# Layer norm of a decoder trunk: the last quarter of seven norms moves from VectorE to ScalarE, and the exponential's table load moves ahead of the copies of the turned tokens

## The chip, the cores and the metric

The kernel runs on one core of a Trainium2 chip. The metric is the device time of one execution in microseconds; of several runs the median counts.

## The reference

Input is x of 256 tokens by 1024 channels in float32. Four layers follow one another. Layer i mixes the tokens (kind i mod 3: gated DeltaNet, differential attention, chunked gMLP, and DeltaNet again in the fourth layer), then a grouped top-2 mixture of 16 experts follows. Each of the eight halves ends in a residual and a layer norm:

```python
def layer_norm(x, g, b):
    mu = jnp.mean(xf, -1, keepdims=True)
    var = jnp.mean(jnp.square(xf - mu), -1, keepdims=True)
    return (xf - mu) * lax.rsqrt(var + EPS) * g + b
...
    h = layer_norm(DN_ALPHA * h + y, ln_mix_g[i], ln_mix_b[i])
    m = grouped_moe(h, w_router, router_bias, e_w1[i], e_w3[i], e_w2[i])
    h = layer_norm(DN_ALPHA * h + m, ln_ffn_g[i], ln_ffn_b[i])
```

The router takes the sigmoid of h times `w_router` per expert, chooses two experts in one group, and the experts are SiLU-gated: `silu(t @ w1) * (t @ w3) @ w2`. All weights are float32; those of one layer's experts are 16 x 3 matrices of 2 MB.

## The kernel before, in words

The 256 tokens lie on the partitions as two tiles of 128 (`tt` 0 and 1), each 1024 channels wide, in the buffer `H`. The eight layer norms are numbered by phase: phases 1, 3, 5 and 7 follow the mixers (called mixer norms here), phases 2, 4, 6 and 8 follow the experts (expert norms). Phase 8 writes the output and has its own code.

A norm is worked in four quarters: two token tiles by two halves of 512 channels. VectorE (DVE) gathers the statistics of a tile (`bn_stats`, L1109 and L1163, then `bn_aggr`, L1116, which signals `var_ready`). ScalarE (ACT) takes the square root (L783 in `ln_rstd`, signal `rstd_ready`). DVE turns it into the reciprocal root with four one-column operations (`root`, L1126 to L1130), each of which waits for the one before through `own.link`. Then `normalise` (L1146) computes (x - mean) * rstd for the two halves. In mixer norms it reads `H` with a stride of 8 elements and writes `XH`, with the channels in another order. In expert norms tile 0 is normalised in place in `H`, and tile 1 is read from the PSUM banks 6 and 7 (where the last expert pass left it) and written to `H`; the signal is then `drained[6]` or `drained[7]` in place of `xhat_ready`.

TensorE (PE) turns the normalised tokens, 128 channels at a time, into the eight banks `ht` (`ht_chunks`; transposes of L1766 in mixer norms and L1754 in expert norms). It waits for a signal at channel chunk 0 and at chunk 4 of each tile. ACT (L764) empties the even chunks and DVE (L1103) the odd ones into `HT`; both multiply by the gain and add the bias of the norm on the way. All of a norm's `HT` is what the next matmuls read.

After a mixer norm the experts stage begins with the router. PE multiplies `HT` by the router weights (L2080, 16 matmuls, each chunk k waiting for the copy of chunk k), ACT copies the result (`rtq`) to SBUF (L1008), PE folds it (L2085), ACT takes the exponential (L1009), and DVE chooses the experts (from L1450 on). SyncE (SP), which issues the weight loads, waits for `rtq` as well ahead of a load into `HT` (L540). ACT's order in this stretch is written out by hand: `ln_rstd(TT)` with a throw-away Sqrt that brings in Sqrt's table (`ahead(ACT.Sqrt)`, L771), the two square roots, `ht_chunks`, then `experts`, which starts with `ahead(ACT.Exp)`: the load of the exponential's table and a throw-away Exp on one column (`warm`), which the next instruction waits for.

After the choice of experts, DVE and PE select the tokens of each expert and PE gathers them (L2099). GpSimd (POOL) writes the normalised tokens out to HBM in the chosen order, and SP brings them back (L572) before it issues further expert weights into slots as PE lets go of them.

After expert norm 2 (the attention layer is next) ACT issues three DMAs in `toeplitz()` between `ln_rstd` and `ht_chunks` (L1000 and twice L1003). They bring the position bias, for which PE waits (`toep_in`) at its first matmul of L1988, in the middle of the attention's input projection (L1775).

Of the kernel before, what the change touches and what calls it, by code (L numbers as in the profile page):

```python
# [22 lines left out]
P = 128  # L23
# [231 lines left out]
def trunk(nc, w, out, kinds=ALL_KINDS, with_moe=True):  # L255
# [3 lines left out]
    with ExitStack() as ctx:  # L259
# [167 lines left out]
        rstd_ready = sem("rstd_ready")  # L427
        xhat_ready = sem("xhat_ready")
        h_ready = sem("h_ready")
        mask_ready = sem("mask_ready")  # L430
        sel_ready = sem("sel_ready")
        spread_set = sem("spread_set")
# [180 lines left out]
        def _(pool):  # L613
# [14 lines left out]
            def residual(phase, which, i):  # L628
                nonlocal ph
                ph += 1  # L630
                pool.wait_ge(rows_in, 32 * ph)
                if phase == last_phase:

                    return
                own.then(pool.tensor_scalar(gB[:, :], gB[:, :], ALPHA, None, ALU.mult))  # L635
                pool.tensor_scalar(bB[:, :], bB[:, :], ALPHA, None, ALU.mult).then_inc(rows_scaled, 1)
                if which and with_moe:

                    pool.wait_ge(spots_ready, i + 1)
                    for n in range(2):  # L640
                        for tt in range(TT):
                            pool.indirect_dma_start(choice_rows, bass.IndirectOffsetOnAxis(ap=spots[:, n * TT + tt:n * TT + tt + 1], axis=0),
                                                    XH[:, tt, :], None).then_inc(rows_out, 16)
                    return
                pool.wait_ge(rows_scaled, ph)
                own.wait()
                if not which:

                    for k in range(KC):
                        wait_data(pool, "ht", phase, k)  # L650
                else:
                    pool.wait_ge(xhat_ready, 6 * i + 4)
                for tt in range(TT):
                    if which:
                        own.then(pool.tensor_tensor(H[:, tt, :].rearrange("t (p k) -> t k p", k=KC), XH[:, tt, :].rearrange("t (k p) -> t k p", k=KC),
                                                    gB[:, :].rearrange("t (p k) -> t k p", k=KC), ALU.mult))
                    else:
                        own.then(pool.tensor_tensor(H[:, tt, :], H[:, tt, :], gB[:, :], ALU.mult))
                own.wait()
                for tt in range(TT):  # L660
                    pool.tensor_tensor(H[:, tt, :], H[:, tt, :], bB[:, :], ALU.add).then_inc(h_ready, 1)
# [68 lines left out]
        def _(act):  # L730
# [41 lines left out]

            rsq = 0

            def ln_rstd(parts=1):

                nonlocal rsq
                ahead(ACT.Sqrt)
                for n in range(parts):
                    ts = slice(n, n + 1) if parts == TT else slice(0, TT)  # L780
                    rsq += 1
                    act.wait_ge(var_ready, rsq)
                    a(rs[:, 0, ts], mv[:, ts, 1], ACT.Sqrt, bias=epsc[:, 0:1]).then_inc(rstd_ready, 1)  # L783

            def heads_root(nn, tt):

# [217 lines left out]
                                  bass.AP(tensor=scratch.tensor, offset=off, ap=[[1, P], [TOEP, HEADS], [1, n]])).then_inc(toep_in, 16)  # L1004

            def experts(i):
                ahead(ACT.Exp)
                emptied(a(logitT, wait_data(act, "rtq", i)[:, 0:SEQ], ACT.Copy), "rtq", i)  # L1008
                emptied(a(rt[:, 0, :], wait_data(act, "rt", i)[:, 0:TT * E], ACT.Exp, scale=-1.0), "rt", i)  # L1009
                wait_copy(act, "rank", i)  # L1010
                first = at[("moe", i)]
                def pair(it, lead):
                    more = GATHER_STEPS if lead else 0
                    counted = [act.value_load(counts[0:1, bass.ds(it * 2 + j, 1)], min_val=0, max_val=SEQ) for j in range(2)]
                    def turned(j):

                        b = 2 + j
                        act.wait_ge(filled[b], it * 3 + (first[b] + 2))
                        a(hT[j], bank[b][:, SEQ:].rearrange("p (m c) -> p m c", m=4), ACT.Copy).then_inc(drained[b], 1)  # L1019

                    for j in range(2):
                        b = 2 + j
                        if j and not lead:
                            turned(0)
                        act.wait_ge(filled[b], it * 3 + (first[b] + 1))
                        a(sil[j][CAP:, :], bank[b][0:CAP, :], ACT.Silu).then_inc(silu_h, 1)  # L1026
                        with act.If(counted[j] > CAP):
                            with act.Fori(1, PASSES) as n:
                                with act.If(counted[j] > n * Q + Q):
                                    b0 = act.snap(steps_done)  # L1030
                                    act.wait_ge(baton, b0 + (more + 2))
                                    a(m_sil[CAP:, 0:SEQ], bank[5][0:CAP, 0:SEQ], ACT.Silu).then_inc(baton, 1)
                                    act.wait_ge(baton, b0 + (more + 5))
                                    a(m_turned[:, 0:SEQ + P], bank[6][:, 0:SEQ + P], ACT.Copy).then_inc(baton, 1)
                                    act.wait_ge(baton, b0 + (more + 7))
                                    a(m_y, bank[7][:, :], ACT.Copy).then_inc(baton, 1)
                                    act.reg_add(steps_done, steps_done, PASS_STEPS + more)
                    for j in range(2):
                        if lead or j:
                            turned(j)  # L1040
                        if lead and j == 0:
                            for k in range(1, KC, 2):
                                ps = wait_data(act, "cg", i, k)
                                if k > 1:
                                    wait_data(act, "cg", i, KC - 1)
                                c = KC * i + k
                                emptied(a(xc[:, k, 0:2 * SEQ], ps[:, :], ACT.Identity, scale=lncols[:, c:c + 1], bias=lncols[:, c + 32:c + 33]), "cg", i, k)
                    for j in range(2):
                        b = 2 + j
                        act.wait_ge(filled[b], it * 3 + (first[b] + 3))  # L1050
                        for nh in range(2):
                            ins = a(y_[CAP * j:CAP * (j + 1), nh * 512:(nh + 1) * 512], bank[b][nh * CAP:(nh + 1) * CAP, :], ACT.Copy)  # L1052
                        ins.then_inc(drained[b], 1)

                pair(0, True)
                with act.Fori(1, E // 2) as it:
                    pair(it, False)
# [6 lines left out]
            for i, kind in enumerate(kinds):  # L1064
                j = kinds[:i].count(kind)
                if kind == 0:
                    delta(i, j, nn)
                    nn += 1
                elif kind == 1:
                    attention(i, j)  # L1070
                    for tt in range(TT):
                        heads_root(nn, tt)
                        heads_out_T(i, tt, lambda n: bOT[:, :, n * P:(n + 1) * P])
                    nn += 1
                else:
                    gmlp(i, j)
                rows_load(2 * i + 1, 1, i)
                ln_rstd(TT)
                if 2 * i + 1 != last_phase:
                    ht_chunks(2 * i + 1)  # L1080
                if with_moe:
                    experts(i)
                    rows_load(2 * i + 2, 0, i)
                    ln_rstd(TT)
                if 1 in kinds[i + 1:i + 2]:
                    toeplitz()
                if i < n_layers - 1:
                    ht_chunks(2 * i + 2)
# [3 lines left out]
        def _(dve):  # L1092
# [42 lines left out]

            def normalise(phase, tt):

                for kh in range(2):
                    dst = src = H[:, tt, kh * 512:(kh + 1) * 512]
                    ready = xhat_ready  # L1140
                    if phase % 2:
# [579 lines left out]
        def _(pe):  # L1721
# [21 lines left out]
            def ht_chunks(phase):  # L1743
                if phase and phase % 2 == 0:
                    i = phase // 2 - 1
                    for tt, ks in ((0, range(6)), (1, range(6)), (0, (6, 7)), (1, (6, 7))):
                        for k in ks:
                            if tt == 0:
                                pe.wait_ge(xhat_ready, 6 * i + 5 + k // 4)
                                fill("ht", phase, k)  # L1750
                            elif k % 4 == 0:
                                b = 6 + k // 4
# [7 lines left out]
                for tt in range(TT):  # L1760
                    if phase == 0:
                        pe.wait_ge(x_ready[tt], 16)
                    for k in range(KC):
                        if phase and k % 4 == 0:
                            pe.wait_ge(xhat_ready, 6 * (phase // 2) + 2 * tt + k // 4 + 1)
                        ins = tr(pss[k][:, tt * P:(tt + 1) * P], src[:, tt, k * P:(k + 1) * P], ident)  # L1766
                        if tt == TT - 1:
                            done(ins, "ht", phase, k)
# [641 lines left out]
```

## Time and profile before

| what | value |
|---|---|
| median of 3 runs | 1864.21 us (1863.75 to 1871.41) |
| span of the profiled execution | 1862.9 us |
| what lies around the span, against the median | 1.3 us |
| PE busy | 1704.4 us, 91% |
| DVE busy | 660.7 us, 35% |
| ACT busy | 456.2 us, 24% |
| POOL busy | 164.6 us, 9% |

The profile is of one execution. Its own total time is not listed apart from the runs', so the span is set beside their median. Starts in the rows are microseconds from the start of the span. "L1146" is a line of the kernel. A busy PE is not PE at its peak. The idle time before an instruction and what released it stand in square brackets.

### The profile page before, as it was taken

How to read it: one execution, taken by the hardware profiler on the slowest of the kernel's cores; microseconds unless marked ns; L12 is line 12 of the kernel's file. 1: busy time of each engine (PE TensorE's matmuls, PEld its weight loads, DVE VectorE, ACT ScalarE, POOL GpSimd, SP SyncE). 2: the span in 40 equal slices, each digit the busy share in tenths (PEclk: the TensorE clock that was granted, in tenths of full speed). 3: DMA queues.
4: the chain of work that ended last, by engine and by line, in shares of the span. 5: the costliest groups of instructions: out<-in, count | busy, mean ns of one | idle time of the engine just before them, and what ended most of it. 6: DMA issues, size and time to landing. Idle time of an engine off the chain costs nothing. (4 is left out here: it accounts for less than half of the span.)

```text
span 1862.9 us, 24394 instructions
## 1 busy us (share of the span) xinstructions
PE 1704.4 (91%) x9154; PEld 880.5 (47%) x9154; DVE 660.7 (35%) x1397; ACT 456.2 (24%) x898; POOL 164.6 (9%) x129
## 2 busy tenths in 40 slices
PE   8998989998898888899999997899989998899986
PEld 7866643332584443333344544333368667433322
DVE  3443563222216552232302225222243435542223
ACT  1674312111204121111211101111124834111111
POOL 1013110000300100000020100000030131200000
PEclk9999989999999989999999998999989999899999
DMA  9431089999943389689974339899993220699996
GB/s 335 178 128 47 24 317 423 421 422 423 386 168 119 109 367 407 269 345 421 403 256 147 113 145 384 369 423 421 423 344 136 91 92 2 250 383 422 422 422 249
DMA packets 107163, 521.87 MB, mean 280 GB/s; under 512 B 10819, under 2 KB 19060, under 8 KB 65788
## 3 DMA queue, kind: packets, MB, share of 16 engines
q1 hardware_dynamic: 93680, 497.05, 66.5%
q10 hardware_dynamic: 11020, 14.07, 2.3%
q0 software_dynamic: 2304, 8.39, 1.1%
q8 instruction: 130, 2.13, 0.5%
q14 instruction: 29, 0.24, 0.0%
HBM read 510.03 MB, written 9.45 MB: 279 GB/s over the span
## 5 line engine op out<-in xcount | busy, mean ns | idle before, releaser
L2112 PE MATMUL bank<-ring,work 128*64 128x512 f32 x1280 | 285.1, 595 | 7.9 <-DMA ring<-in_e_w 7.9
L1618 DVE TENSOR_TENSOR work<-bank,work 64x512 f32<-64x512 f32 x64 | 68.0, 1063 | 530.6 <-ACT work L1026 530.5
L1775 PE MATMUL bank<-HT,ring 128*128 128x256 f32 x1024 | 231.4, 386 | 0.0
L2156 PE MATMUL bank<-ring,work 128*64 128x512 f32 x896 | 206.8, 603 | 12.1 <-DMA ring<-in_e_w 9.8
L1775 PEld LDWEIGHTS bank<-HT,ring 128*128 128x128 f32 x1024 | 198.4, 194 | 37.0 <-issue 10.2
L1783 PE MATMUL bank<-ring,HT 128*128 128x512 f32 x448 | 197.9, 601 | 0.0
L2112 PEld LDWEIGHTS bank<-ring,work 128*64 128x64 f32 x1280 | 88.5, 137 | 176.6 <-issue 160.7
L1026 ACT ACTIVATE work<-bank 64x512 f32<-64x512 f32 x64 | 37.7, 589 | 428.0 <-PE bank L2112 428.0
L1783 PEld LDWEIGHTS bank<-ring,HT 128*128 128x128 f32 x448 | 85.9, 194 | 103.8 <-issue 103.8
L2156 PEld LDWEIGHTS bank<-ring,work 128*64 128x64 f32 x896 | 61.7, 138 | 133.5 <-issue 111.2
L2189 PE MATMUL bank<-work 128*128 128x512 f32 x256 | 119.7, 611 | 5.2 <-DVE H L1641 5.2
L635 POOL TENSOR_SCALAR gB<-gB 128x1024 f32<-128x1024 f32 x7 | 20.1, 2867 | 1036.1 <-DMA bB<-in_ln_ffn_b 716.6
L1052 ACT ACTIVATE work<-bank 64x512 f32<-64x512 f32 x128 | 75.7, 592 | 130.5 <-PE bank L2156 129.8
L1249 DVE SCALAR_TENSOR_TENSOR work<-bank,convcols,work 128x255 f32<-128x255 f32 x144 | 69.3, 482 | 103.3 <-ACT work L829 99.9
L2112 PE MATMUL bank<-work 128*64 128x512 f32 x320 | 101.0, 593 | 3.8 <-DMA work<-in_e_w 2.7
L1808 PE MATMUL bank<-ring,work 128*128 128x512 f32 x192 | 84.2, 597 | 0.0
L2189 PEld LDWEIGHTS bank<-work 128*128 128x128 f32 x256 | 46.9, 192 | 77.4 <-issue 69.4
L2112 PE MATMUL bank<-early_slot,work 128*64 128x512 f32 x320 | 72.2, 593 | 2.6 <-DMA early_slot<-in_e_w 2.6
L1569 DVE TENSOR_TENSOR H<-bank,H 128x512 f32<-128x512 f32 x112 | 70.1, 684 | 6.3 <-PE bank L2189 5.2
L1019 ACT ACTIVATE work<-bank 128x256 f32<-128x256 f32 x64 | 24.6, 384 | 173.3 <-PE bank L2120 173.2
L2112 PEld LDWEIGHTS bank<-work 128*64 128x64 f32 x320 | 30.9, 137 | 69.3 <-issue 61.1
L2112 PE MATMUL bank<-HT,work 128*64 128x512 f32 x128 | 57.6, 593 | 0.0
(318 smaller groups left out, 1798.1 us busy)
## 6 DMA issues: line engine op xcount, KB each, us to landing
ring<-in_e_w SPq DMA_DIRECT2D x160, 1024.0 KB, 18.5
ring<-in_e_w SPq DMA_DIRECT2D x56, 2048.0 KB, 21.2
early_slot<-in_e_w SPq DMA_DIRECT2D x40, 1024.0 KB, 18.2
work<-in_e_w SPq DMA_DIRECT2D x40, 1024.0 KB, 19.4
ring<-in_a_w_in SPq DMA_DIRECT2D x15, 2048.0 KB, 19.7
HT<-in_e_w SPq DMA_DIRECT2D x16, 1024.0 KB, 20.6
work<-in_e_w SPq DMA_DIRECT2D x8, 2048.0 KB, 22.7
ring<-in_c_w_in SPq DMA_DIRECT2D x8, 2048.0 KB, 22.6
```

Source lines behind the costliest of these rows:

```text
L1019: a(hT[j], bank[b][:, SEQ:].rearrange("p (m c) -> p m c", m=4), ACT.Copy).then_inc(drained[b], 1)
L1026: a(sil[j][CAP:, :], bank[b][0:CAP, :], ACT.Silu).then_inc(silu_h, 1)
L1052: ins = a(y_[CAP * j:CAP * (j + 1), nh * 512:(nh + 1) * 512], bank[b][nh * CAP:(nh + 1) * CAP, :], ACT.Copy)
L1249: ins = v.scalar_tensor_tensor(dst[:, back:SEQ], ps[:, 0:SEQ - back], convcols[:, j, col:col + 1], dst[:, back:SEQ], ALU.mult, ALU.add)
L1569: v.tensor_tensor(part(b), bank[b][:, :], part(b), ALU.add).then_inc(drained[b], 1)
L1618: v.tensor_tensor(by_m(h_[j]), bank[b][CAP:, :], sil[j][CAP:, :], ALU.mult).then_inc(drained[b], 1)
L1775: ins = mm(dst[:, 0:SEQ], wt[:, k, n * P:(n + 1) * P], HT[:, k, :], start=k == 0, stop=k == KC - 1)
L1783: ins = mm(dst[:, :], HT[:, k, tt * P:(tt + 1) * P], wt[:, k, :], start=k == 0, stop=k == KC - 1)
L1808: ins = mm(ps[:, :], turned(h, tt), wts[nh][:, h, :], start=h == 0, stop=h == HEADS - 1)
L2112: ins = mm(bank[b][lo:lo + CAP, :], x[:, k, :], wt[k], start=k == 0, stop=k == KC - 1, skip_group_check=True)
L2156: ins = mm(bank[b][nh * CAP:(nh + 1) * CAP, :], h[:, m, :], w2[m][:, nh * 512:(nh + 1) * 512], start=m == 0, stop=m == 3, skip_group_check ...
L2189: mm(bank[b][:, :], selgT[:, tt * P:(tt + 1) * P], y_[:, nh * 512:(nh + 1) * 512], start=tt not in onto_h, stop=True, skip_group_check=tt ...
```

## The change

For the phases 1 to 7 the last quarter (tile 1, channels 512 to 1023) is normalised by ACT. DVE computes -mean * rstd of tile 1 in one more one-column operation and signals it as `shift_ready`. ACT waits for it and does Identity(x * rstd + shift) over 512 channels right behind the second square root. In mixer norms it signals the new semaphore `xhat_last`, in expert norms `drained[7]`. PE's and POOL's waits are counted anew. The throw-away Exp with its table load moves from the start of `experts` to the place between `ln_rstd` and `ht_chunks` of the mixer norms. Phase 8 stays as it was.

```diff
-            def ln_rstd(parts=1):
+            def ln_rstd(parts=1, phase=None):
...
                     a(rs[:, 0, ts], mv[:, ts, 1], ACT.Sqrt, bias=epsc[:, 0:1]).then_inc(rstd_ready, 1)
+                    if phase is not None and n:
+                        second_half(phase)
+
+            def second_half(phase):
+
+                act.wait_ge(shift_ready, phase)
+                if phase % 2:
+                    dst = XH[:, 1, 512:].rearrange("t (k p) -> t k p", p=P)
+                    src, ready = H[:, 1, :].rearrange("t (p k) -> t k p", k=KC)[:, 4:, :], xhat_last
+                else:
+                    dst, src, ready = H[:, 1, 512:], bank[7][:, :], drained[7]
+                a(dst, src, ACT.Identity, scale=rs[:, 3, 1:2], bias=rs[:, 2, 1:2]).then_inc(ready, 1)
...
             def experts(i):
-                ahead(ACT.Exp)
...
                 rows_load(2 * i + 1, 1, i)
-                ln_rstd(TT)
+                ln_rstd(TT, 2 * i + 1)
+                ahead(ACT.Exp)
                 if 2 * i + 1 != last_phase:
                     ht_chunks(2 * i + 1)
                 if with_moe:
                     experts(i)
                     rows_load(2 * i + 2, 0, i)
-                    ln_rstd(TT)
+                    ln_rstd(TT, 2 * i + 2 if 2 * i + 2 != last_phase else None)
...
             def normalise(phase, tt):

-                for kh in range(2):
+                if tt:
+                    v.scalar_tensor_tensor(rs[:, 2, 1:2], mv[:, 1, 0:1], -1.0, rs[:, 3, 1:2], ALU.mult, ALU.mult).then_inc(shift_ready, 1)
+                for kh in range(1 if tt else 2):
...
                         if phase and k % 4 == 0:
-                            pe.wait_ge(xhat_ready, 6 * (phase // 2) + 2 * tt + k // 4 + 1)
+                            if (tt, k) == (1, 4):
+                                pe.wait_ge(xhat_last, phase // 2 + 1)
+                            else:
+                                pe.wait_ge(xhat_ready, 5 * (phase // 2) + 2 * tt + k // 4 + 1)
```

## Rows read from the trace of the kernel before

**Rows 1.** The page: the span.

```profile
span 1862.9 us, 24394 instructions
```

**Rows 2.** Chain that ended last, phase 7: start us, us, what.

```profile
1607.38 0.75 DVE work L1146
1608.13 0.04 issue
...
1608.69 1.94 ACT HT L764 x4
...
1610.64 1.16 ACT L771
...
1612.17 0.39 ACT work L1008
```

**Rows 3.** Timelines of DVE, ACT and SP in phase 3.

```profile
648.63 0.16 DVE L1130 SCALAR_TENSOR_TENSOR rs<-rs 128x1 f32<-128x1 f32 x1
648.83 1.41 DVE L1146 TENSOR_SCALAR work<-H,mv,rs 128x512 f32<-128x512 f32 x2
650.14 1.90 DVE L1103 TENSOR_SCALAR HT<-bank,lncols 128x256 f32<-128x256 f32 x4
...
649.99 1.93 ACT L764 ACTIVATE HT<-bank,lncols 128x256 f32<-128x256 f32 x4 [1.98 <-PE bank L1766]
651.94 1.28 ACT L771 ACT_TABLE_LOAD   x1
653.47 0.38 ACT L1008 ACTIVATE work<-bank 128x256 f32<-128x256 f32 x1
...
652.74 0.33 SPq L540 DMA_DIRECT2D HT<-in_e_w  x1
```

**Rows 4.** The same timelines in phase 1, and DVE's tile 0 there.

```profile
232.12 2.82 DVE L1146 TENSOR_SCALAR work<-H,mv,rs 128x512 f32<-128x512 f32 x2
...
245.79 1.41 DVE L1146 TENSOR_SCALAR work<-H,mv,rs 128x512 f32<-128x512 f32 x2
247.31 1.90 DVE L1103 TENSOR_SCALAR HT<-bank,lncols 128x256 f32<-128x256 f32 x4
...
250.58 0.38 ACT L1008 ACTIVATE work<-bank 128x256 f32<-128x256 f32 x1
...
250.48 0.33 SPq L540 DMA_DIRECT2D HT<-in_e_w  x1
```

**Rows 5.** Timelines of DVE and SP in phase 7.

```profile
1608.90 1.90 DVE L1103 TENSOR_SCALAR HT<-bank,lncols 128x256 f32<-128x256 f32 x4
...
1611.78 0.33 SPq L540 DMA_DIRECT2D HT<-in_e_w  x1
```

**Rows 6.** Stretches: us, busy of PE, PEld, DVE, ACT, POOL, PEclk, DMA share, GB/s.

```profile
260.00:264.00 4.00, 4.00 (x25) 4.00 (x24) 1.99 (x11) 1.28 (x1) 2.05 (x2) 0.62 0.66 271
...
268.00:272.00 4.00, 4.00 (x22) 1.38 (x20) 2.26 (x15) 0.00 (x0) 0.00 (x0) 1.00 0.60 210
...
272.00:400.00 128.00, 126.01 (x580) 45.44 (x578) 40.72 (x60) 24.35 (x44) 0.00 (x0) 1.00 1.01 420
```

**Rows 7.** Groups of instructions by line, ACT: 512 columns from PSUM, scale and bias per partition.

```profile
L1047 ACT ACTIVATE work<-bank,lncols 128x512 f32<-128x512 f32 x16 | 11.6, 775 | 18.3 <-PE bank L2200 18.3
```

**Rows 8.** Timelines of DVE and PE in phase 2.

```profile
491.46 1.53 DVE L1146 TENSOR_SCALAR H<-bank,mv,rs 128x512 f32<-128x512 f32 x2
...
492.32 2.40 PE L1754 MATMUL bank<-consts_sb,H 128*128 128x128 f32 x10 [1.05 <-DVE H L1146]
```

**Rows 9.** The position bias: ACT's queue, the DMA's landing, PE's first use.

```profile
489.94 0.34 ACTq L1000 DMA_DIRECT2D work<-in_consts  x1
490.31 1.25 ACTq L1003 DMA_DIRECT2D work<-toeplitz_rows  x2
...
work<-toeplitz_rows ACTq DMA_DIRECT2D x1, 1024.0 KB, 20.1
...
512.08 1.02 PE L1988 MATMUL bank<-work 128*128 128x512 f32 x2
```

More of the change, by code:

```diff
@@ L429, in trunk @@
         h_ready = sem("h_ready")
+        shift_ready = sem("shift_ready")
+        xhat_last = sem("xhat_last")
         mask_ready = sem("mask_ready")
@@ L651, in residual @@
                 else:
-                    pool.wait_ge(xhat_ready, 6 * i + 4)
+                    pool.wait_ge(xhat_ready, 5 * i + 3)
+                    pool.wait_ge(xhat_last, i + 1)
                 for tt in range(TT):
@@ L1748, in ht_chunks @@
                             if tt == 0:
-                                pe.wait_ge(xhat_ready, 6 * i + 5 + k // 4)
+                                pe.wait_ge(xhat_ready, 5 * i + 4 + k // 4)
                                 fill("ht", phase, k)
```

## The prediction

> **What bounds the kernel now.** I first read the page for the span, 1862.9 us [rows 1], then the chain of waits that ended last, to see whether a layer norm stands in it and by which instructions. It does. In phase 7 the chain goes from VectorE's quarter (L1146) over PE's turn to ScalarE's four copies (L764), then to the table load (L771), then to the copy of the router's result (L1008) [rows 2]. So ScalarE, not VectorE, is the engine that holds this stretch from the first turned chunk on, and the table load stands in the chain.
>
> The timelines show how much of that load is exposed. L1008 needs two things: the router's last matmul, whose end SP shows (it waits for the same signal ahead of its load into HT), and ScalarE free. In phase 3 the matmuls end at 652.74 and L1008 starts at 653.47: the load costs 0.73 us less a hand-over of 0.04, so 0.69 [rows 2, 3]. Phase 5 repeats phase 3 to within 0.01. In phase 1 it is 250.58 - 250.48 - 0.04 = 0.06 [rows 4], in phase 7 1612.17 - 1611.78 - 0.04 = 0.35 [rows 2, 5]. All four together expose 1.8 us of the 5.1 us that four loads take; the rest lies under the router's matmuls.
>
> Does a delay here reach the end? After the router, the choice of experts, the gather and the return of the gathered rows follow in one chain, and SP lets go of further weights only behind it. DMA is not backlogged then: 0.60 busy in 268 to 272. From 272 on it is full at 420 GB/s [rows 6], and moves the start of that stretch along with the router. I therefore pass every delay on in full, in mixer norms as in expert norms, behind which PE works without a gap.
>
> **The change, part by part.** S is the start of VectorE's third quarter (first of tile 1), right behind the last step of `root`: 245.79, 648.83 and 1607.38 in phases 1, 3 and 7 [rows 2 to 4].
>
> *The added one-column operation.* It is of the kind of L1130, 0.16 us [rows 3]. It stands ahead of the third quarter. VectorE overlaps neighbours a little when none waits: two quarters take 1.41, though one is 0.75, so 0.09 overlap [rows 2, 3]. That gives 0.07 at least, and 0.20 (the pitch from L1130 at 648.63 to 648.83) at most. I take 0.10, nearest the unlinked case that this is. PE's first turn starts that much later.
>
> *The quarter taken off VectorE.* Its end is what PE waits for at chunk 4. In expert norms PE starts the turns at 492.32 and VectorE ends the quarter at 492.99 [rows 8]; ten turns take 2.40, so the four ahead of chunk 4 take 0.96, more than the 0.67 between. In mixer norms ScalarE's copies, 1.93 for four, are slower than the turns that feed them [rows 3]. VectorE's own next work, the odd copies, starts during the quarter's last 0.1 us or right behind it [rows 3, 8] and isn't last. I cost the gain at nothing: under the quarter lie PE's four turns. If they were gone it would be worth 0.66.
>
> *ScalarE's quarter in mixer norms.* It starts at S + 0.16 + 0.04. The trace has no Identity from SBUF with this stride. Nearest is L1047, the same function, width and operands from PSUM: 0.775 [rows 7]. From above, VectorE's quarters of the same strided tile: 0.75, and 1.41 each in their slowest pair (2.82) [rows 4]. I take 0.80, as ScalarE's own row is nearest. It ends at S + 1.00, just ahead of PE's chunk 4. In expert norms, with PSUM as source, 0.775 fits as it stands, and behind it stand only the copies, which wait for PE, and in phase 2 three DMAs (below).
>
> The Trainium skill speaks against the strided read ("SBUF - State Buffer", the notes on SBUF cachelines): accesses that cross to a new 16-byte line pay a penalty, and here each step is 32 bytes. No row shows it for ScalarE.
>
> *The moved table load.* This is the large term. It can't start before ScalarE's quarter is done, and the copies wait behind it: quarter to S + 1.00, load 1.28, then 0.25 to the next instruction (in phase 3 from 651.94 + 1.28 to 653.47) [rows 3]. The first copy starts at S + 2.54 in place of S + 1.16 (649.99 - 648.83). The four copies take 1.93, so the last ends at S + 4.47. Then the router's last matmuls must still run: from the last copy (VectorE's, 652.04) to 652.74 are 0.70 us in phase 3; 1.27 in phase 1 (249.21 to 250.48) and 0.98 in phase 7 (1610.80 to 1611.78) [rows 3 to 5]. L1008 then starts at:
> phase 1: 245.79 + 4.47 + 1.27 + 0.04 = 251.57, later by 0.99;
> phase 3: 648.83 + 4.47 + 0.70 + 0.04 = 654.04, later by 0.57; phase 5 the same;
> phase 7: 1607.38 + 4.47 + 0.98 + 0.04 = 1612.87, later by 0.70.
> Sum 2.8 us. The load that was mostly hidden under the router's matmuls now stands in front of what they need. The bounds are 2 (matmuls catching up) and 3.5.
>
> On the price of a load the Trainium skill ("ScalarE: Activation LUTs", What ACT_TABLE_LOAD costs) gives 1283 ns plus 1380 ns of drain. The trace agrees on the first (1.28) and shows no drain: the next instruction starts 0.25 later, itself included. By the page the sum would be up to 4 x 1.38 = 5.5 us more.
>
> *Expert norms.* Three times the 0.10 ahead of PE's first turn: 0.3.
>
> *Order of ScalarE's queue in phase 2.* The three position-bias DMAs were issued from 489.94 to 491.56. Now they are behind the wait for `shift_ready`: from 491.46 + 0.16 + 0.04 = 491.66, so 1.72 later. They hold up the copies of phase 2 by some 0.4, hidden under the turns still to come. But PE needs the bias at 512.08, and the large DMA, issued between 490.31 and 491.56, takes 20.1 to land: 510.4 to 511.7 [rows 9]. 1.72 later it lands at 512.1 to 513.4. Since PE has slipped by 0.1, the wait is 0 to 1.3; I take the middle, 0.7. Other transfers share the engines then, so it may land less late.
>
> **Sum.** 2.8 + 0.3 + 0.7 = 3.8 us on the span of 1862.9. The median of the runs is 1.3 above the span, so 1864.2 + 3.8 = 1868.0. That is 0.2%. A measurement of this kernel tells about 0.5%, 9.3 us, from no change (the three runs lie 7.7 us apart), so my forecast is no change that shows, leaning to slower.
>
> **The rivals.**
> *The load hides, as the move suggests.* If ScalarE had room for it before PE's first turned chunk is there, the exposed 1.8 would be saved, and VectorE's added operation would still cost 0.3 in the expert norms: 1864.2 - 1.8 + 0.3 = 1862.7. Against it: ScalarE's idle time ahead of the copies is 1.98 us in all [rows 3], but the quarter cuts it in two, and only S + 1.00 to S + 1.16 lies behind the quarter. 0.08.
> *The strided quarter is slow.* 1.41 in place of 0.80 delays load and copies four times by 0.6, and PE's chunk 4 with it: 1870.4. For it the stride; against it the flat rows of ScalarE. 0.12.
> *The delay is absorbed.* The bias lands in time and the router's matmuls catch up: 1865.5. 0.15.
> *Slower by more than shows: the clock.* PE would idle up to 1.4 us more between its turns and the router. In 260 to 264 the granted clock is 0.62, so between half and full speed [rows 6], and phase 1's router tail at 1.27 against phase 3's 0.70 prices a low clock at about half speed. If the low clock lasts longer behind each idle spell, PE's work costs double for as long. To add the missing 5.5 us it must last some 2.8 us longer at each of four norms, with PE busy at half speed in twice that. Against it: the idle time of the expert choice is far longer and decides anyway. 1874 and more. 0.04.
> *It does not do what it says*: another table load for Identity. No: Identity follows Sqrt without one in every norm [rows 3]. Under 0.01.
>
> **How the numbers follow.** My forecast has 0.60; with the absorbed case and the slow quarter 0.87 lies between 1864 and 1872. The range goes from 1862.0, which takes in most of the gain, to 1872.0: the slow quarter, and a long bias wait. Of the three signs: faster by over 0.5% would need 9.3 us, while all four loads and seven quarters together are 5.1 + 5.3 = 10.4; 0.02. Slower by over 0.5%: the clock, and 0.01 for what no row shows, 0.05. Within 0.5%: 0.93.
>
> **What would show it.** In the profile after: ScalarE's quarter of 0.8 us at S + 0.2, the load right behind it, the first copy at S + 2.5, no gap at L1008 other than PE's, and 0.6 to 1.0 more from S to L1008 in the four mixer norms. A wait for DMA at PE's first L1988. I am wrong if the copies start near S + 1.2, if the quarter takes over 1.0, or if the span grows while these intervals don't.

## The result and the profile after

The changed kernel takes 1872.3 us (median of 11 runs, 1870.2 to 1879.4); the kernel before, run beside it, 1866.1 us. The ratio is 1.0032, 95% interval 1.0019 to 1.0046: the change costs 6.0 us (3.5 to 8.6). The spans of the two profiled executions are 5.6 us apart, 1868.5 against 1862.9. The forecast was 1868.0 us, 3.8 us slower, with 1872.0 as the upper end. Sign and place were right, the size was not. (Where a whole time is given in us against before, below too, it is worked out from the ratio of the runs.)

Phase 3 shows the change at work. The line of the span on its profile page and the timelines of VectorE, ScalarE, PE and SP in the changed kernel:

```profile
span 1868.5 us, 24401 instructions
...
653.01 0.16 DVE L1141 RECIPROCAL rs<-rs 128x1 f32<-128x1 f32 x1 [0.36 <-ACT rs L786]
...
653.79 0.16 DVE L1154 SCALAR_TENSOR_TENSOR rs<-mv,rs 128x1 f32<-128x1 f32 x1
653.87 0.73 DVE L1163 TENSOR_SCALAR work<-H,mv,rs 128x512 f32<-128x512 f32 x1
...
653.99 1.31 ACT L798 ACTIVATE work<-H,rs 128x512 f32<-128x512 f32 x1 [1.01 <-DVE rs L1154]
655.32 1.28 ACT L774 ACT_TABLE_LOAD   x1
656.62 0.20 ACT L774 ACTIVATE warm<-epsc 128x1 f32<-128x1 f32 x1
656.85 1.93 ACT L767 ACTIVATE HT<-bank,lncols 128x256 f32<-128x256 f32 x4
659.95 0.38 ACT L1022 ACTIVATE work<-bank 128x256 f32<-128x256 f32 x1 [1.17 <-PE bank L2100]
...
654.66 1.35 PE L1786 MATMUL bank<-consts_sb,work 128*128 128x128 f32 x8 [1.66 <-DVE work L1163]
657.92 1.98 PE L2100 MATMUL bank<-HT,wr 128*32 128x256 f32 x16 [1.91 <-ACT HT L767]
...
659.95 0.33 SPq L542 DMA_DIRECT2D HT<-in_e_w  x1
```

These answer to [rows 3]. Before, the four copies (L764, now L767) started 1.16 us behind S, as soon as PE had turned the first chunk. Now the quarter (L798, 1.31), the load (1.28) and the throw-away Exp stand in front of them, and PE idles 1.91 us between its turns and the router. Where the copy of the router's result used to wait for the load, it now waits 1.17 us for PE.

To compare kernels I measure from R, the start of VectorE's reciprocal for tile 1, to that copy (L1008, now L1022). In phase 3 it is 659.95 - 653.01 = 6.94 us, and it was 653.47 - 648.04 = 5.43. The table gives all kernels that matter; every number in it is a difference of two starts in the timelines of one profiled execution of each kernel, and the last column adds the four norms' differences to before. The kernels of the last three rows have e1's order of ScalarE in their mixer norms.

| kernel | phase 1 | 3 | 5 | 7 | sum against before |
|---|---|---|---|---|---|
| before | 5.57 | 5.43 | 5.43 | 5.57 | |
| changed | 6.95 | 6.94 | 6.94 | 6.95 | +5.8 |
| table load alone (e1) | 5.36 | 4.71 | 4.70 | 5.12 | -2.1 |
| quarter alone (e2) | 5.66 | 5.65 | 5.66 | 5.66 | +0.6 |
| load ahead of the quarter (e4) | 5.94 | 5.94 | 5.93 | 5.93 | +1.7 |
| two more switches (e8) | 9.97 | 9.97 | 9.97 | 9.98 | +17.9 |
| expert quarter alone (e6) | 5.14 | 5.48 | 4.71 | 5.24 | -1.4 |
| GpSimd later (e7) | 5.09 | 5.47 | 4.71 | 5.29 | -1.4 |
| e7 again (e11) | 5.07 | 5.48 | 5.13 | 5.29 | -1.0 |

The chain that ended last in phase 7 has the same order now (changed kernel; start us, us, what):

```profile
1611.50 0.17 DVE rs L1154
...
1611.69 1.06 ACT work L798
1612.75 0.29 issue
1613.04 1.28 ACT L774
1614.32 0.01 issue
1614.33 0.21 ACT warm L774
1614.54 0.03 issue
1614.57 1.03 ACT HT L767 x2
1615.60 0.04 issue
1615.64 2.00 PE bank L2100 x16
1617.64 0.02 issue
1617.67 0.39 ACT work L1022
```

In [rows 2] VectorE's quarter and PE's first turn led to the copies and the load came behind them. Now quarter, load and copies are one series on ScalarE, and the router's matmuls have joined it.

The groups of instructions give ScalarE's quarter by its two forms, from SBUF in the mixer norms and from PSUM in the expert norms (changed kernel: busy us, mean ns of one | idle before):

```profile
L798 ACT ACTIVATE work<-H,rs 128x512 f32<-128x512 f32 x4 | 5.3, 1322 | 4.0 <-DVE rs L1154 4.0
L798 ACT ACTIVATE H<-bank,rs 128x512 f32<-128x512 f32 x3 | 2.3, 777 | 5.6 <-DVE rs L1154 5.6
```

From PSUM it takes 0.777, as [rows 7] had it. From SBUF with the stride it takes 1.32. In phase 4 PE's turns of tile 1 begin 1.71 us behind R, where they began at 1.65: 0.06 for the added operation. Phase 2 lost 0.74 there; that is taken up below.

The 5.8 of the four norms lies close to the 6.0 of the whole time, but two executions don't make a ledger. At R the changed kernel's profile is 9.5 us behind the one of before in phase 5 (1121.79 against 1112.29) and 4.1 in phase 7 (1610.72 against 1606.60). From the one R to the other it took 5.4 us less than before, though its norm of phase 5 alone costs 1.5 more, so other stretches vary by more than the whole change costs. That a norm's delay reaches the end rests on the medians, and on e8.

### The profile page after: what moved, and what is told of

Its sections match the earlier page's. It is cut to its first block and busy times, and to the rows that moved or that the text cites. A ratio compares the mean times of both kernels' runs of the same rounds, so it can differ in the third digit from the quotient of the medians.

```text
span 1868.5 us, 24401 instructions
## 1 busy us (share of the span) xinstructions
PE 1710.0 (92%) x9154; PEld 884.5 (47%) x9154; DVE 656.4 (35%) x1397; ACT 463.6 (25%) x905; POOL 165.1 (9%) x129
## 5 line engine op out<-in xcount | busy, mean ns | idle before, releaser
L1828 PEld LDWEIGHTS bank<-ring,work 128*128 128x128 f32 x192 | 36.8, 195 | 45.1 <-issue 45.1
```

The lines of the kernel that those rows point to most:

```text
L1828: ins = mm(ps[:, :], turned(h, tt), wts[nh][:, h, :], start=h == 0, stop=h == HEADS - 1)
```

## The experiments

Three things were open: whether the moved load, the quarter or something outside ScalarE costs the 6 us; why the quarter takes 1.32; and how much of a delay in a norm reaches the end. Line numbers are those of each kernel; the times of before that were measured beside them are 1867.0 us for e1 to e4, 1867.2 for e5 to e8 and 1865.7 for e9 to e11.

### e1: the table load alone

```diff
                 rows_load(2 * i + 1, 1, i)
                 ln_rstd(TT)
+                ahead(ACT.Exp)
...
             def experts(i):
-                ahead(ACT.Exp)
```

(against the kernel before)

> The kernel before with the table load alone moved; VectorE keeps all quarters. R is the start of VectorE's reciprocal for tile 1 (root); from R to the copy of the router's result (L1008) the kernel before takes 5.57, 5.43, 5.43 and 5.57 us in phases 1, 3, 5 and 7, the changed kernel 6.94 to 6.95 in all four. Theory A (series on ScalarE: whatever stands between the second square root and the copies counts only if it lasts beyond PE's first turned chunk): the load fits into ScalarE's idle time behind the second square root, the copies start as before, and L1008 comes at R + 5.5, 4.75, 4.75, 5.2; four norms save 1.8 us, the time is 0.1% under before. Theory B (the moved load itself is what costs): L1008 at R + 6 or later, time 2 to 6 us above before. Theory C (clock and DMA, not ScalarE's order, made the difference): R to L1008 says nothing, the time is near that of the changed kernel.

1866.2 us, ratio 0.9993 (0.9977 to 1.0008). ScalarE's timeline in phase 3:

```profile
647.21 0.29 ACT L783 ACTIVATE rs<-mv,epsc 128x1 f32<-128x1 f32 x1 [13.38 <-DVE mv L1116]
647.52 1.28 ACT L771 ACT_TABLE_LOAD   x1
648.81 0.20 ACT L771 ACTIVATE warm<-epsc 128x1 f32<-128x1 f32 x1
649.54 1.93 ACT L764 ACTIVATE HT<-bank,lncols 128x256 f32<-128x256 f32 x4 [0.52 <-PE bank L1766]
652.24 0.38 ACT L1007 ACTIVATE work<-bank 128x256 f32<-128x256 f32 x1 [0.77 <-PE bank L2080]
```

The load starts right behind the second square root, and ScalarE is done with it and the throw-away Exp 0.52 us before PE's first turned chunk lets the copies start. L1008 comes at R + 5.36, 4.71, 4.70 and 5.12: 2.1 us saved over four norms in this execution, where 1.8 were expected. Theories B and C fall: the move costs nothing by itself, and this half of the change is a small gain. As a whole time it can't be told from nothing.

The 2.1 is the best of four executions. e6, e7 and e11 have the same mixer norms and save 1.4, 1.4 and 1.0 (table). With ScalarE out of the way, the copy of the router's result waits for PE alone, and so for PE's clock. In phase 3 of e11 the router's matmuls ran at a granted clock of 0.50 (first line: stretch in us, busy of PE, PEld, DVE, ACT, POOL, granted clock, DMA share, GB/s), and the copy (L1008, there L1010) came at R + 5.48, later than before:

```profile
654.00:655.94 1.94, 1.93 (x17) 0.78 (x16) 0.73 (x2) 0.60 (x2) 0.00 (x0) 0.50 0.91 389
...
656.00 0.38 ACT L1010 ACTIVATE work<-bank 128x256 f32<-128x256 f32 x1 [1.40 <-PE bank L2083]
```

### e2: the quarter alone

```diff
                 ln_rstd(TT, 2 * i + 1)
-                ahead(ACT.Exp)
...
             def experts(i):
+                ahead(ACT.Exp)
```

(this and the following, unless said otherwise, against the changed kernel)

> The changed kernel with the table load put back to the start of the experts stage; ScalarE keeps the last quarter. Theory A: quarter from R + 0.97 to R + 2.30, copies R + 2.33 to R + 4.26, then load and throw-away Exp, L1008 at R + 5.8: 1.15 us less than the changed kernel in each of four norms, 0.2 to 0.4 more than before; time 4.6 us under the changed kernel, 1 to 2 above before. Theory B: the same or larger gain over the changed kernel, equal to before. Theory D (the quarter alone costs): as slow as the changed kernel, L1008 at R + 6.9.

1868.3 us, ratio 1.0006 (0.9991 to 1.0021); L1008 at R + 5.65 to 5.66 in all four norms, 1.29 less than in the changed kernel. The series theory (theory A) said 5.8. Theory D, that the quarter alone costs it all, falls. The quarter by itself delays the copies by 0.1 to 0.25 us (they start at R + 2.20; before at 1.95 to 2.09). So neither half costs what both do: the quarter ends at R + 2.30, after PE's first chunk is there, and it keeps the load out of the idle time in which e1 hides it.

### e3: a quarter without the stride

```diff
-                    dst = XH[:, 1, 512:].rearrange("t (k p) -> t k p", p=P)
-                    src, ready = H[:, 1, :].rearrange("t (p k) -> t k p", k=KC)[:, 4:, :], xhat_last
+                    dst, src, ready = XH[:, 1, 512:], H[:, 1, 512:], xhat_last
```

> The changed kernel, but ScalarE's quarter in mixer norms reads and writes its 512 channels one after another instead of with a stride of 8 (so the channels of that quarter come in another order than the router and experts need). Theory A: the quarter takes 0.80 instead of 1.33, the load and all behind it start 0.53 earlier, L1008 at R + 6.4, time 2.1 us under the changed kernel. Rival (the quarter is long because ScalarE and VectorE read the same rows of SBUF at once): the quarter stays at 1.3 and nothing moves. The experts see other values, so the choice of experts and the number of extra passes may differ; the norm's intervals are what counts.

ScalarE's timeline in phase 3:

```profile
654.36 0.81 ACT L797 ACTIVATE work<-H,rs 128x512 f32<-128x512 f32 x1 [1.01 <-DVE rs L1153]
655.19 1.28 ACT L774 ACT_TABLE_LOAD   x1
656.49 0.20 ACT L774 ACTIVATE warm<-epsc 128x1 f32<-128x1 f32 x1
656.72 1.93 ACT L767 ACTIVATE HT<-bank,lncols 128x256 f32<-128x256 f32 x4
```

The quarter takes 0.81 in all four mixer norms, and L1008 comes at R + 6.44, both as the series theory said. VectorE still reads the same rows at the same time, so that rival falls. The write was in a row already (XH's 512 channels, chunk by chunk), so the read is all that this edit changes for the quarter: 4 x 128 channels 32 bytes apart against 512 in a row. It costs 0.51. This kernel gives the router the quarter's channels in the wrong order, so that other experts are chosen: PE's matmuls are 8730 in place of 9154. The whole time (1834.0 us, ratio 0.9815) therefore says nothing here.

### e4: the load ahead of the quarter

```diff
                     if phase is not None and n:
+                        if phase % 2:
+                            ahead(ACT.Exp)
                         second_half(phase)
...
                 ln_rstd(TT, 2 * i + 1)
-                ahead(ACT.Exp)
```

> The changed kernel, but the exponential's table load stands ahead of ScalarE's quarter instead of behind it, in the idle time while VectorE finishes the root. Theory A: load R to R + 1.3, quarter R + 1.5 to R + 2.85, copies R + 2.9 to R + 4.8, L1008 at R + 5.5 to 6.0: about 1.2 less than the changed kernel in each of four norms, time 4 to 5 us under it. PE's chunk 4 waits 0.5 to 1 longer for the quarter, under ScalarE's copies. Theory B: the place makes no difference, L1008 at R + 6.9.

1868.6 us, ratio 1.0000 (0.9986 to 1.0013). L1008 at R + 5.93 to 5.94, 1.00 less than in the changed kernel. The quarter now runs from R + 1.52 to 2.84, since it waits for the throw-away Exp, and the copies start at R + 2.74. One swap of two statements gives back 4 us of the change's cost in the norms, and the whole time can't be told from before.

### e5: the bias DMAs ahead of the quarter

```diff
                     rows_load(2 * i + 2, 0, i)
-                    ln_rstd(TT, 2 * i + 2 if 2 * i + 2 != last_phase else None)
+                    ln_rstd(TT)
                 if 1 in kinds[i + 1:i + 2]:
                     toeplitz()
+                if 2 * i + 2 != last_phase:
+                    second_half(2 * i + 2)
```

> The changed kernel, but in phase 2 ScalarE issues the three position-bias DMAs ahead of its wait for shift_ready, as before, and does the quarter behind them. R2 is the start of VectorE's reciprocal for tile 1 of phase 2. From R2 to PE's first matmul with the bias (L1988 before, L2008 changed) the kernel before took 21.4 us, the table-only kernel 20.9, every kernel with the late issue 23.3 to 23.7. Theory E (the late issue costs twice: the bias lands late, and the rows of the next norm land earlier in its place, so that GpSimd's scaling meets VectorE's root, whose L1128 took 0.82 to 0.89 there instead of 0.16): R2 to the first bias matmul falls to 21 to 21.6, GpSimd starts its scaling near R2 + 1.4, no wait for DMA, time 2 us under the changed kernel. Rival F (ScalarE's quarter and the shift on VectorE are what lengthens phase 2): it stays at 23 or more. The mixer norms stay at R + 6.94.

1876.2 us, ratio 1.0047 (1.0030 to 1.0064): not faster than the changed kernel, where 2 us less were expected. R2 to the first bias matmul stayed at 23.44 us, and GpSimd's scaling stayed at R2 + 0.00. Theory E falls. The wait for the bias had been there in the changed kernel, and is gone here. This is the line of the changed kernel (PE's waits from 490 to 520 us: in total, times, longest):

```profile
PE bank L2008 <- DMA work<-toeplitz_rows: 0.5, 1, 0.5
```

But it was 0.5 us of the 2.06 that this stretch had grown by. Another 0.74 is the later start of PE's turns, behind VectorE's root (e7 below). The last 0.8 is clock. The stretches of PE's turns and of its matmuls up to the bias, kernel before and then changed kernel (us, busy of PE, PEld, DVE, ACT, POOL, granted clock, DMA share, GB/s):

```profile
490.37:494.51 4.14, 3.09 (x16) 2.90 (x17) 3.92 (x10) 1.48 (x3) 2.41 (x1) 0.66 1.05 384
494.51:512.08 17.57, 17.57 (x81) 15.44 (x81) 1.87 (x5) 3.59 (x7) 12.41 (x6) 0.98 1.07 370
```

```profile
491.59:496.47 4.88, 3.73 (x16) 3.28 (x17) 3.95 (x10) 2.06 (x4) 4.59 (x2) 0.50 1.05 386
496.47:515.36 18.89, 18.36 (x82) 15.69 (x81) 2.35 (x5) 4.06 (x9) 10.24 (x5) 0.95 1.07 371
```

The same 80 matmuls kept PE busy 0.8 us longer, because full clock (2.4 GHz) came back later. The granted clock was still 0.50 for the first microsecond of the changed kernel's projection, where before it averaged 0.70 over that microsecond; it was 1.00 from 1 us on before, from 2 us on in the changed kernel and from 4 us on in e5. How long the low one (1.2 GHz) lasts behind the expert stage differs from execution to execution: the stretch from PE's first projection matmul to the bias took 17.3 in e1, 17.6 before, 18.5 in e6, and 18.9 in e5, in e9 and, with the 0.5 of wait, in the changed kernel. e5 lost in clock what it saved in waiting.

### e6: ScalarE's quarter in the expert norms alone

```diff
-                ln_rstd(TT, 2 * i + 1)
+                ln_rstd(TT)
                 ahead(ACT.Exp)
...
-                if tt:
+                if tt and phase % 2 == 0:
...
-                for kh in range(1 if tt else 2):
+                for kh in range(1 if tt and phase % 2 == 0 else 2):
```

(against e5, with the counts of the waits as before)

> ScalarE's quarter in the expert norms alone (phases 2, 4, 6), with the bias DMAs ahead of it; in mixer norms VectorE keeps all four quarters and the table load stands behind the second square root, as in the table-only kernel. Theory A: the mixer norms are those of the table-only kernel (L1008 at R + 4.7 to 5.4), each expert norm costs 0.08 for the added operation, time within 0.3 us of the table-only kernel. Rival (the quarter in the expert norms is what gains): 0.6 to 2 us under the table-only kernel.

1868.1 us, ratio 0.9994 (0.9980 to 1.0007), beside e1's 0.9993. PE's turns of tile 1 begin at R + 1.71 in phases 2 and 4, where e1 has 1.64 and 1.65. The added operation costs 0.06 to 0.07, and the quarter's move brings PE's start of the turns no nearer, as the series theory said. The median was 1.8 us above e1's, though, and a difference within 0.3 us is more than these runs can show.

### e7 and e11: GpSimd's scaling later

```diff
                     return
+                if not which:
+                    for k in range(KC):
+                        wait_data(pool, "ht", phase, k)
                 own.then(pool.tensor_scalar(gB[:, :], gB[:, :], ALPHA, None, ALU.mult))
```

(against e1)

> The table-only kernel, and in expert norms GpSimd waits for the turned chunks before it scales the gain and bias rows (it waits for them right behind the scaling as it is). Theory E: the scaling no longer meets VectorE's root in phase 6; L1128 there takes 0.16 instead of 0.84, the norm is 0.7 shorter and nothing waits for GpSimd; time 0.7 us under the table-only kernel. Rival G (GpSimd's rows are needed soon, so the delay comes back at the next residual): VectorE waits for h_ready, time as before or above. With the table load's 1.8 to 2.1 us: 2.5 to 2.8 us under before, 0.14%.

e7 took 1865.5 us, ratio 0.9990 (0.9979 to 1.0000). The mechanism is plain in phase 6. VectorE's second root step in the kernel before, with GpSimd's scaling beside it, and then in e7:

```profile
1369.41 2.77 POOL L635 TENSOR_SCALAR gB<-gB 128x1024 f32<-128x1024 f32 x1 [236.28 <-DMA bB<-in_ln_ffn_b]
1369.60 0.86 DVE L1128 SCALAR_TENSOR_TENSOR rs<-mv,rs 128x1 f32<-128x1 f32 x1
```

```profile
1373.37 0.16 DVE L1131 SCALAR_TENSOR_TENSOR rs<-mv,rs 128x1 f32<-128x1 f32 x1
1377.41 2.77 POOL L638 TENSOR_SCALAR gB<-gB 128x1024 f32<-128x1024 f32 x1 [241.24 <-PE bank L1757]
```

The second root step starts at R + 0.19 in both. GpSimd's scaling began at R before and at R + 4.23 in e7. PE's turns of tile 1 begin at R + 1.64 in place of 2.34, which is the 0.7 us expected. The whole time is 0.1% under before. I ran it again to see whether that was real:

> The table-only kernel with GpSimd's late scaling once more: 0.999 of before again (0.998 to 1.000), that is 1.5 to 2.8 us; the turns of tile 1 at R + 1.64 in all three expert norms. If the 0.999 was chance, it comes out between 0.9995 and 1.001.

1865.0 us, ratio 1.0007 (0.9990 to 1.0024), with the turns at R + 1.64 in all three expert norms. By what was set down, the 0.999 was chance, though the two intervals overlap. The gain in the norm is there each time, a gain in whole time is not shown.

### e8: two more table switches

```diff
                 ahead(ACT.Exp)
+                ahead(ACT.Sqrt)
+                ahead(ACT.Exp)
```

> The changed kernel with two more table switches (Sqrt, then Exp, each a load of 1.28 and a throw-away of 0.25) behind the moved one, in each mixer norm: ScalarE's copies start 3.05 us later. It measures how much of a delay in a mixer norm reaches the end. If all of it (as the prediction had it): L1008 at R + 10.0 and 4 x 3.05 = 12.2 us over the changed kernel, 18 over before, 1.0%. If weight transfers that limit the experts stage absorb part: R + 10.0 all the same, but 5 to 9 us over the changed kernel.

1887.1 us, ratio 1.0099 (1.0079 to 1.0118); L1008 at R + 9.97 to 9.98. The four norms are 4 x 3.03 = 12.1 us longer than in the changed kernel, and 17.9 longer than before. The whole time is 18.5 us above before (14.8 to 22.0), 12.5 above the changed kernel's 6.0. A delay in a mixer norm reaches the end in full, within some 4 us. Had 5 to 9 of the 12.1 been all that arrived, the whole would lie 11 to 15 above before, which only the low end of the interval touches.

### e9 and e10: the changed kernel again, and the mixer quarters alone

```diff
-                    ln_rstd(TT, 2 * i + 2 if 2 * i + 2 != last_phase else None)
+                    ln_rstd(TT)
...
-                if tt:
+                if tt and phase % 2:
...
-                for kh in range(1 if tt else 2):
+                for kh in range(1 if tt and phase % 2 else 2):
```

(e10, which also counts its wait for `shift_ready` anew; e9 has no edit)

> The changed kernel once more, on the chip of the two runs beside it: the ratio to before again at 1.003 (1.002 to 1.005); from the last root step on, L1008 at R + 6.94 in all four mixer norms. Theory A has no other value for it.

1872.2 us, ratio 1.0032 (1.0017 to 1.0046), L1008 at R + 6.93 to 6.94.

> The changed kernel with VectorE doing all quarters in the expert norms again; ScalarE keeps the mixer quarters and the load behind them. Theory A: L1008 at R + 6.94, expert norms as before but for GpSimd: PE's turns of tile 1 begin at R + 1.64 in phase 4 in place of 1.71. What is open: in phase 2 GpSimd's scaling began at R2 + 1.4 in the three kernels without ScalarE's mixer quarter and at R2 in the six with it, which costs PE's turns 0.7 us through VectorE's root. If the mixer quarter is what goes with it: R2 + 0.0 here and the turns at R2 + 2.3. If the expert quarter does: R2 + 1.4 and the turns at R2 + 1.64. Time in both cases within 1 us of the changed kernel, 5 to 6 us above before.

1874.6 us, ratio 1.0042 (1.0026 to 1.0058), its median 2.4 us above e9's where at most 1 was expected, with intervals that overlap. L1008 at R + 6.94 and 6.95, the turns at R + 1.64 in phase 4. In phase 2 GpSimd began at R2 + 0.01, as it should if the mixer quarter is what goes with it. But e9, the very program of the changed kernel, had it at R2 + 1.40, where the changed kernel's first profile had it at R2 - 0.03. So it isn't bound to either quarter: it differs from one execution to the next, though the load of the rows that GpSimd waits for is issued at R2 - 8.48 before and in both profiles of the changed kernel. What decides its landing stays open. The 0.7 us that phase 2 lost in the first profile is not a fixed part of the change.

## Why the prediction was wrong

**The step that failed** is the price of ScalarE's quarter in mixer norms, 0.80 us, taken from the row with the same function, width and operands but read from PSUM [rows 7]. It measured 1.32. Read in a row from SBUF it measured 0.81 (e3), so the price was right for a read that this kernel doesn't make. Four norms at 0.52 make 2.1 of the 3.0 us that the norms' sum lacked (5.8 measured, 2.8 forecast). The prediction had named a quarter over 1.0 as a sign of being wrong. The Trainium skill's note on SBUF cachelines ("SBUF - State Buffer"), weighed in the prediction, says that such a read pays a penalty; e3 agrees for ScalarE, 1.32 against 0.81.

The trace of before shows two things that bear on this and that I had missed. VectorE's own quarters show a price of the stride: in expert norms it reads tile 0 in a row from SBUF (and writes it in place), in 0.518 us a quarter, against the 0.75 of the strided one.

```profile
L1146 DVE TENSOR_SCALAR H<-H,mv,rs 128x512 f32<-128x512 f32 x6 | 2.9, 518 | 0.0
```

And the upper bound of 1.41, from VectorE's slowest pair [rows 4], was near the truth by luck. That pair, from 232.12 to 234.94, ran while GpSimd scaled its rows:

```profile
230.44 2.77 POOL L635 TENSOR_SCALAR gB<-gB 128x1024 f32<-128x1024 f32 x1 [38.75 <-DMA bB<-in_ln_mix_b]
233.17 3.02 POOL L636 TENSOR_SCALAR bB<-bB 128x1024 f32<-128x1024 f32 x1
```

Of the eight such pairs in the kernel before, the three beside GpSimd take 1.99 to 2.82, and the five without it 1.40 to 1.41.

**The rest is the router's matmuls.** For the time from the last copy to L1008 I took what it was before, 1.31, 0.74, 0.74 and 1.02 in phases 1, 3, 5 and 7 with the hand-over. It is now 1.17 in all four (658.78 to 659.95 in phase 3). Phases 1 and 7 cancel, and phases 3 and 5 add 0.43 each, some 0.9 us. The granted clock in the stretch of the router's matmuls fell in phase 3 from 1.00 before to 0.71 in the changed kernel, behind 1.91 us of idle PE:

```profile
651.06:652.71 1.65, 1.65 (x16) 0.78 (x16) 0.98 (x3) 1.63 (x3) 0.00 (x0) 1.00 0.92 392
```

```profile
657.92:659.90 1.98, 1.98 (x16) 0.49 (x16) 0.00 (x0) 0.86 (x2) 0.00 (x0) 0.71 1.06 451
```

e2 has the same quarter but no such idle time, and there the same 16 matmuls take 1.54 at full clock:

```profile
653.63:655.17 1.54, 1.54 (x16) 0.45 (x16) 0.77 (x2) 1.52 (x3) 0.00 (x0) 1.00 0.95 404
```

The other profiles say the same. Where PE's turns ran at 1.00 and the router followed within 0.3 us, the router ran at 1.00 too (seven norms of before, e1, e2, e6 and e7). Where PE idled 1.9 us or more between them, the router ran at 0.50 to 0.71 (five norms of the changed kernel, e5, e8 and e10). The clock stood among the rivals with a chance of 0.04 and a price of 5.5 us more; in the norms it came with a sixth of that price.

**Point by point.** The load in ScalarE's series and its 1.28 + 0.25: right, and e1, e2 and e4 move it as the sum would. The exposed 1.8 us before: right for that trace, e1 saves 2.1 at best and 1.0 where PE's clock is low. The added operation at 0.10: measured 0.06 to 0.07. VectorE's saved quarter worth nothing: nothing shows against it, and in the expert norms PE starts no earlier (e6). Delays pass on in full: right within some 4 us (e8). The late bias, 0 to 1.3 us, taken as 0.7: a wait of 0.5 in one profile and none in e9, where PE itself was later by its clock. That is inconclusive as a cost, and moving the DMAs back gained nothing (e5). With the measured quarter and router the sum would have been 5.8 + 0.2 for the expert norms + up to 0.5 = 6.0 to 6.5; the runs show 6.0 (3.5 to 8.6). The absorbed case at 1865.5 doesn't follow from its own terms, 2 + 0.3, which make 1866.5; nothing rests on it.

**The range.** The time came 0.3 us above its upper end. The base moved: the kernel before took 1866.1 us in 11 runs, 1.9 above the three that were shown. I had seen that those lay 7.7 us apart and left the base out of the range. On the base that was shown, a cost of 6.0 would have ended at 1870.2, inside the range, and that would have been luck, since the quarter's price was wrong all the same. The upper end took the slow quarter together with a long bias wait, but not with the clock, which is what came with it.

**No version beats the kernel before by what can be measured.** e1 has the change's useful half and is the one to keep if any: 1.0 to 2.1 us less in the four norms by four profiles, ratio 0.9993 with 1 inside its interval.

## What to carry to other kernels

Ahead of a table load that is to hide in an engine's idle time, put no work that has to wait for another engine: here the load was free right behind the square root, and behind the quarter it cost its full length (1.29 us a norm, from e2 to the changed kernel). When work is moved to another engine, price it by that engine's rows with the same memory and the same stride; if there is none, let the unlike row be the end of a range and not its middle. Look also for what the same stride costs any engine that has rows with it and without. And add the rivals that can come together, and the spread of the base, before closing a range.

## What was unexpected of the hardware

ScalarE took 1.32 us for 512 float32 read from SBUF 32 bytes apart and 0.81 for the same read in a row (e3); VectorE's quarter of the same strided tile took 0.73 at that time, against 0.52 for a quarter read in a row in the expert norms. A one-column VectorE operation that normally takes 0.16 took 0.80 to 0.90 when GpSimd began a 1024-column scaling some 0.2 us before it. That happened in phase 6 of every kernel in which GpSimd wasn't held back, and in phase 2 of seven profiles, and the four-step root hands it to PE in full. The one-column operations that follow while the same scaling still runs take 0.16 again.
